# A two-layer decoder trunk on one core: order of two adding transfers, and how far ScalarE and VectorE prepare weights ahead inside the feed-forward units

## The reference, cut to what matters

```
hn = rms_norm(h, norm_ffn_g[layer])
h = h + (silu(hn @ ffn_w_gate[layer]) * (hn @ ffn_w_up[layer])) @ ffn_w_down[layer]     # 1024 -> 2816 -> 1024
```

## Time and profile before

| | us |
|---|---|
| median of 3 runs | 558.1 (558.05 to 558.82) |
| the profiled execution's own time | 559.87 |
| its span, first to last instruction | 558.0 |
| mean granted TensorE clock | 0.999 of full speed |
| PE busy / VectorE busy / ScalarE busy | 548.7 / 474.1 / 348.9 |

### The profile page before, as it was taken

How to read it: one execution, slowest core, us unless ns; L and a number is a source line. 1 busy time by engine, 2 the same in 40 slices (tenths; PEclk the granted TensorE clock), 3 DMA queues, 4 the chain that set the end, 5 groups by cost and what they waited for, 6 DMA issues and landing times.

```text
span 558.0 us, 7380 instructions
## 1 busy us (share of the span) xinstructions
PE 548.7 (98%) x2805; PEld 461.0 (83%) x2805; DVE 474.1 (85%) x564; ACT 348.9 (63%) x475; POOL 29.0 (5%) x70
## 2 busy tenths in 40 slices
PE   8999999999999999999999999999999999999996
PEld 7899978887888788888888888888788888878785
DVE  5769996798989999878798998977989898989765
ACT  6877664664767486655666366646576666748524
POOL 1200001100000010000000000001010000000000
PEclk9999999999999999999999999999999999999999
DMA  8995546845979879774469422409789697977102
GB/s 295 409 404 196 189 150 211 270 123 132 298 258 286 307 203 340 189 286 167 151 256 346 174 76 76 151 29 292 284 221 339 187 314 243 295 284 211 56 0 75
DMA packets 32867, 122.42 MB, mean 219 GB/s; under 512 B 3648, under 2 KB 4800, under 8 KB 30784
## 3 DMA queue, kind: packets, MB, share of 16 engines
q1 hardware_dynamic: 30384, 105.04, 49.8%
q0 software_dynamic: 2304, 16.78, 15.7%
q10 hardware_dynamic: 144, 0.14, 0.1%
HBM read 120.89 MB, written 1.05 MB: 219 GB/s over the span
## 4 chain that ended last, share of the span: by engine, by line
PE 71%; DVE 16%; DMA 5%; issue 4%; ACT 3%; POOL 0%; SPq 0%; DVEq 0%; ACTq 0%; POOLq 0%
PE bank L1792 12%; PE bank L1794 12%; PE bank L1793 12%; DVE w_lo L1133 7%; PE bank L2266 5%; PE bank L2265 5%; PE bank L2270 5%; PE bank L1903 4%; PE bank L2237 3%; DMA spare<-in_slabs 2%; DMA sixth_raw<-in_slabs 2%; PE bank L1906 2%; DVE raw L1597 2%; PE bank L2242 1%; ACT w_hi L682 1%
## 5 line engine op out<-in xcount | busy, mean ns | idle before, releaser
L1133 DVE TENSOR_TENSOR w_lo<-raw,w_hi 128x2048 fp32r<-128x2048 f32 (+2 forms) x71 | 156.2, 2211 | 21.5 <-ACT w_hi L682 21.0
L682 ACT ACTIVATE w_hi<-raw 128x2048 fp32r<-128x2048 f32 (+2 forms) x66 | 120.8, 1846 | 5.0 <-DMA raw<-in_slabs 2.8
L1792 PE MATMUL bank<-w_lo,yT_hi 128*128 128x512 f32 (+1 forms) x226 | 91.3, 404 | 2.2 <-DVE yT_lo L1690 1.6
L1794 PE MATMUL bank<-w_hi,yT_lo 128*128 128x512 f32 (+1 forms) x226 | 88.1, 390 | 0.0
L1793 PE MATMUL bank<-w_hi,yT_hi 128*128 128x512 f32 (+1 forms) x226 | 87.8, 389 | 0.0
L1133 DVE TENSOR_TENSOR w_lo<-sixth_raw,w_hi 128x2048 fp32r<-128x2048 f32 x22 | 50.3, 2285 | 5.0 <-ACT w_hi L682 5.0
L1792 PEld LDWEIGHTS bank<-w_lo,yT_hi 128*128 128x128 f32 x226 | 42.5, 188 | 13.1 <-DVE yT_lo L1690 4.2
L2265 PE MATMUL bank<-w_hi,forms_hi 128*128 128x512 f32 x128 | 50.4, 394 | 0.0
L1794 PEld LDWEIGHTS bank<-w_hi,yT_lo 128*128 128x128 f32 x226 | 42.4, 188 | 9.1
L2266 PE MATMUL bank<-w_hi,forms_lo 128*128 128x512 f32 x128 | 49.9, 390 | 0.0
L1793 PEld LDWEIGHTS bank<-w_hi,yT_hi 128*128 128x128 f32 x226 | 42.6, 189 | 7.4
(11 more groups left out here) (289 smaller groups left out, 1136.5 us busy)
## 6 DMA issues: line engine op xcount, KB each, us to landing
raw<-in_slabs SPq DMA_DIRECT2D x146, 512.0 KB, 7.7
sixth_raw<-in_slabs SPq DMA_DIRECT2D x28, 512.0 KB, 7.6
sixth_raw<-in_slabs POOLq DMA_DIRECT2D x6, 1024.0 KB, 11.3
spare<-in_slabs SPq DMA_DIRECT2D x12, 512.0 KB, 4.9
raw<-in_slabs POOLq DMA_DIRECT2D x6, 1024.0 KB, 8.8
spare<-in_slabs POOLq DMA_DIRECT2D x4, 1024.0 KB, 10.4
raw<-in_slabs SPq DMA_DIRECT2D x5, 256.0 KB, 4.6
h<-in_x SPq DMA_DIRECT2D x2, 512.0 KB, 6.7
```

The source lines that it names most:

```text
L682: A(w_of(s, c), raw_of(r, c), ACT.Copy).then_inc(hi_ready, 1)
L1133: V.tensor_tensor(w_of(s, c, 1), raw_of(preps[s][0], c), w_of(s, c).bitcast(F32), ALU.subtract).then_inc(lo_ready, 1)
L1792: T.matmul(o, st_hi, mv_lo, start=first, stop=False, skip_group_check=onto)
L1794: return T.matmul(o, st_lo, mv_hi, start=False, stop=last, skip_group_check=onto)
```

## The change

Three edits. GpSimd's program becomes third(2), third(4), fourth(2), third(6), fourth(4), third(8), fourth(6), fourth(8) in each layer, and the thirds count on two semaphores in turn. ScalarE rounds two more slabs (the down slab and T1) before the first unit, and in each unit works two slabs further ahead. VectorE takes T3's low part of the first unit after the activations' low part, takes the low part of the down slab before the first `seven_add`, and in units that have a follower puts `seven_add(a, 1)`, the next B11's low part and `block_add(a + 2, 0)` ahead of gates 0 and 1, and the next T3's and T2's low parts and `block_add(a + 2, 1)` ahead of `seven_add(a, 2)` and gate 3.

```
                 if (kind, a, b) in (("norm", 1, 1), ("norm", 3, 1)):
-                    for unit in SEVEN_AT[a // 2]:
-                        add_third(a // 2, unit)
-                        add_fourth(a // 2, unit)
+                    l, units = a // 2, SEVEN_AT[a // 2]
+                    add_third(l, units[0])
+                    for unit, following in zip(units, units[1:]):
+                        add_third(l, following)
+                        add_fourth(l, unit)
+                    add_fourth(l, units[-1])
...
                 at_hi_evac(3, 1, 1, 1)
+                next_hi(2)
...
                     seven_copy(a, 0)
-                    next_hi(2)
-                    if follows:
-                        seven_hi(a - 2, 3)
+                    next_hi()
                     seven_copy(a, 1)
-                    next_hi(4)
+                    next_hi(3)
                     seven_copy(a, 2)
+                    if leads:
+                        next_hi(2)
                     seven_silu(a, 0)
-                    if leads:
-                        next_hi()
                     seven_silu(a, 1)
                     seven_hi(a, 0)
                     seven_silu(a, 2)
-                    if leads:
-                        seven_hi(a, 1)
-                        next_hi(2)
-                        seven_silu(a, 3)
-                        seven_hi(a, 2)
-                        return
                     next_hi()
                     seven_hi(a, 1)
                     seven_hi(a, 2)
...
                 block_add(SEVEN_AT[l][0], 0)
-                split_los(f + 6)
                 activate(3, 1)
                 at_lo_evac(2, 0, 0, 1)
+                split_los(f + 6)
                 split_forms()
...
                     next_lo()
                     if follows:
-                        seven_act_lo(a - 2, 2)
                         seven_act_lo(a - 2, 3)
-                    next_lo(4)
+                    next_lo(5)
                     seven_add(a, 0)
-                    next_lo()
-                    seven_gate(a, 0)
                     if leads:
                         next_lo()
+                        seven_add(a, 1)
+                        seven_gate(a, 0)
+                        block_add(a + 2, 0)
+                        seven_gate(a, 1)
+                        seven_act_lo(a, 0)
+                        seven_gate(a, 2)
+                        next_lo()
+                        seven_act_lo(a, 1)
+                        next_lo()
+                        block_add(a + 2, 1)
+                        seven_add(a, 2)
+                        seven_gate(a, 3)
+                        seven_act_lo(a, 2)
+                        return
+                    seven_gate(a, 0)
                     seven_add(a, 1)
                     seven_gate(a, 1)
                     seven_act_lo(a, 0)
                     seven_gate(a, 2)
-                    if leads:
-                        block_add(a + 2, 0)
-                        seven_act_lo(a, 1)
-                        seven_add(a, 2)
-                        next_lo(2)
-                        seven_gate(a, 3)
-                        block_add(a + 2, 1)
-                        return
```

More of the change, by code:

```diff
@@ L370, in trunk @@
         block_sum = sem("block_sum")
-        third_added = sem("third_added")
+        third_added = [sem(f"third_added{i}") for i in range(2)]
         fourth_added = sem("fourth_added")
@@ L473, in trunk, with third_sum @@
         SUMS = ("t2", "t1")
+        def third_sum(l, a):
+            n = seven_no(l, a)
+            return third_added[n % 2], 16 * (n // 2) + 16
         sum_of_prep = {}
@@ L476, in trunk @@
             for a in SEVEN_AT[l]:
-                sum_of_prep[place["t3", l, a]] = (third_added, 16 * seven_no(l, a) + 16)
+                sum_of_prep[place["t3", l, a]] = third_sum(l, a)
                 sum_of_prep[place["t4", l, a]] = (fourth_added, 16 * seven_no(l, a) + 16)
@@ L638, in add_third @@
                 pool.wait_ge(raw_loaded[y], made)
-                nc.gpsimd.dma_start(raw_of(y), piece(n, 0, SLAB), accum_op=ALU.add).then_inc(third_added, 16)
+                nc.gpsimd.dma_start(raw_of(y), piece(n, 0, SLAB), accum_op=ALU.add)\
+                    .then_inc(third_sum(l, a)[0], 16)
             def add_fourth(l, a):
@@ L1032, in seven @@
                 def seven(a):
-                    follows, leads = a - 2 in SEVEN_AT[l], a + 2 in SEVEN_AT[l]
+                    leads = a + 2 in SEVEN_AT[l]
                     seven_copy(a, 0)
-                    next_hi(2)
-                    if follows:
-                        seven_hi(a - 2, 3)
+                    next_hi()
                     seven_copy(a, 1)
-                    next_hi(4)
+                    next_hi(3)
                     seven_copy(a, 2)
+                    if leads:
+                        next_hi(2)
                     seven_silu(a, 0)
-                    if leads:
-                        next_hi()
                     seven_silu(a, 1)
@@ L1591, in block_add @@
                     if m == 0:
-                        dve.wait_ge(third_added, 16 * seven_no(l, a) + 16)
+                        dve.wait_ge(*third_sum(l, a))
                     else:
```

## The result

The changed kernel is slower: 568.71 us (median of 4 runs, 567.52 to 569.05) against 558.46 of the kernel before on the same chip, a ratio of 1.0169 (95% interval 1.0147 to 1.0191). The sign of the forecast held and its size did not: 560.7 was forecast with 557.2 to 563.5 as range. The profiled execution has a span of 567.3 against 558.0, and a mean granted clock of 0.991 against 0.999.

A forecast was written before the change was run, and what follows sets the result against it. PE, busy 98% of the span, was taken as the bound, with only its stalls to win. Terms -1.32 - 2.03 + 5.0 + 1.0 = +2.65 us on 558.1 gave 560.7, range 557.2 to 563.5.

The forecast's parts named there:

- How long?: Layer 1's first unit: fourth(2), held behind third(4), lands at 419.95 instead of 416.55, so T4 is rounded 3.4 late.
- no slack to swallow them: Layer 1's first unit: the 3.4 come fully on top, as turn 0 is only just in time without them.
- Later fourths aren't held: Fourths after each layer's first: the next unit's third lands by 160 to 163, and fourth(4) is due at 163.
- the moved low part: Ahead of each layer's first unit: VectorE takes the activations' low part before T3's; 0.66 gained twice, -1.32.
- the late thirds' stall in layer 1: Third(8) of layer 1 no longer waits for a fourth to land; its stall of 1.41 goes.
- unit 6 of layer 0 and unit 4 of layer 1: Units 4 and 6: VectorE's new order makes quarter 0's low part 0.2 late; 0.25 a unit, +1.0 over both layers.
- the first unit's lateness without a hold: First unit of each layer: VectorE, in its new order after T4, delivers the low part 0.8 late to PE.
- ScalarE's lead at nothing: ScalarE rounding two slabs ahead issues the same roundings and slots allow it; costed at nothing.
- The long hold: Rival: both held transfers of layer 1 go at the thirds' pace, T4 8.5 late; +7.75, 565.85; chance 0.08.
- The short hold: Rival: both transfers of layer 1 take 7.8, T4 is 1.5 late; +0.75, 558.85; chance 0.22.
- the faster case: Rival: adding transfers land quickly, third(4) in 6.3 or less, so no hold; 557.35, or 555.75 if fourths are quick too; chance 0.12.
- VectorE late in every unit: Rival: the chain from copy 2 on VectorE takes 0.5 more in six units, 3 more; 563.7; chance 0.08.

The follow-up runs named there:

- two transfers in flight: The changed kernel with GpSimd's transfer scratch at 1024 instead of 512 and six small tiles moved: 565.21 us, 1.0090 against the kernel before.
- GpSimd's order alone: The kernel before with only the new order of thirds and fourths and the two semaphores: 562.72 us (561.2 to 569.09 over 11 runs), 1.0086.
- ScalarE's new order alone: The kernel before with the moved low part and, in layer 0 only, thirds ahead and ScalarE's new order, VectorE's order old: 571.72 us, 1.0214.

## Why the prediction was wrong

**The mechanism was right.** GpSimd gets no second adding transfer out before the one ahead has landed (0.23 after it, 0.25 taken), in whichever order; third(4) waits for its y and fourth(2) behind it; T4's rounding waits on ScalarE, and PE at B22 behind copy 2 and then at turn 0. With twice the scratch fourth(2) left before third(4) had landed: that the scratch holds it is shown by an experiment, not only argued.

**The step that failed is the size of the hold, "How long?"**, taken at 3.4 with 8.5 as its end. Measured against layer 0's first unit, which isn't held, T4 came 22.31 - 12.95 = 9.36 later, and the unit was 41.23 - 31.88 = 9.35 longer: "no slack to swallow them" was exact. The missing 6.0 add up from four figures: third(4) left at 404.12, not 402.2 (+1.9), as y's load, issued at 389.4 to 389.8, took up to 13.9 where the earlier trace rows had 12.9; it took 10.5, not 8.0 (+2.5), with a load that started 0.3 behind it, while in three runs in which that load started 1.5 behind it third(4) took 8.6 to 8.8; fourth(2) took 11.9, not 9.5 (+2.4); and the unheld T4 is 0.8 later than taken (404.42 + 12.95 = 417.37, not 416.55). I had given third(4) the fourths' time since "the queue has just run dry", and fourth(2) the slowest of theirs. But the fourths of the earlier trace rows had a start over the loads, and the held one hadn't: before, in layer 1, it left at 408.44, loads followed at 412.28 and 414.48, and it took 7.8; after, loads left at 411.31 and 413.51, ahead of it, and one at 415.71. The rule of round robin between queues (the Trainium skill, "DMA: Bandwidth & Descriptors", section on queues, rings and completion order), which I weighed and set aside, gave with the earlier trace rows an estimate of 11.5 for this transfer, and the trace's 11.9 is nearer to that than to my 9.5. It doesn't tell the cases apart, though: with loads that started 1.3 or more behind them, such transfers took only 7.8 to 10.1.

**"Later fourths aren't held" failed in layer 0.** Y of unit 6 was there at 155.9, not at 151; third(6) left then, and fourth(4) was held to 164.11 and landed 9.6 later. The new order has no room for that: unit 4 has +0.36 where -0.62 + 0.25 = -0.37 was summed.

**Terms that held:** the moved low part, -0.66 and -0.65 for twice -0.66; the late thirds' stall in layer 1, -1.26 for -1.41 + 0.25; unit 6 of layer 0 and unit 4 of layer 1, +0.17 and +0.19 for 0.25 each; the first unit's lateness without a hold, +1.06 for 0.8. ScalarE's lead at nothing can't be told as a term of its own: the two engines' orders stand or fall together.

Term by term the misses add up: 6.0 for the hold, 2 x 0.26 for first units, 0.73 for layer 0's unit 4, and -0.24 over the other three units, some +7.0; with +2.65 that is the +9.6 of the table.

**Rivals.** The long hold (+7.75, chance 0.08) was the nearest, and also too small. The short hold and the faster case are refuted: no adding transfer of these runs landed in less than 7.7, and the two that the hold is made of took 10.5 and 11.9. The Trainium skill, "DMA: Bandwidth & Descriptors", section on the anatomy of one DMA, would give an estimate of 4.4 us for such a transfer; no run here shows such a time for an adding one. VectorE late in every unit is refuted by units of 31.17 to 31.21.

**Open:** why fourth(2) took 9.4 with only the end of one load beside it, where others with as much took 7.7 to 8.3; why the steady units are 0.2 longer with two transfers in flight; what the four longer runs of GpSimd's order alone lost; and whether layer 1 could gain with y loaded earlier, which wasn't tried.

## What to carry to other kernels

Two transfers of one queue whose triggers are far apart are not independent: moving the one with the later deadline ahead is free only where its own input is there early, as in layer 0 with the old orders and not in layer 1. When a transfer is held, cost it at the speed it has at its new time, beside the loads that then run, and not at the time it used to take. And before tightening an order, read from the trace how late its input comes (here up to 14.15 after B11 was free in the old orders and up to 12.3 in the new); the slack that looks idle may be what absorbs the transfers' spread.

## What the runs showed of the hardware

- The time of an adding transfer of 1 MB goes with the loads around it, over all 208 in the thirteen traces. With no load beside it, or only one that landed within 3.0 of its start, it took 7.7 to 8.3 (9.4 once); with loads that start 1.3 or more after it, 7.8 to 10.1; with a load that starts within 1.3 of it, or that was out before it and landed 4.0 or more after its start, 10.5 to 12.9.
- With a scratch of 512 one such transfer is in flight; with 1024 two are (409.99 went out while the one of 403.90 landed at 412.7). They still land one behind another: in six pairs the first took 7.9 to 8.8, and the second landed 6.9 to 8.0 behind it, so the second took up to 12.5, and 15.1 once, from its issue.
- The granted clock fell after stops of PE of 7.22, 6.48, 5.17, 3.04 and 2.04 to its level of 1.2 GHz (0.51 in the window of after above), and stayed at 1.00 after stops of 3.39 and 1.84. After the same stop of 1.94 in three units of one run (ScalarE's new order alone) it fell in one and stayed in two. So the length of the stop alone doesn't decide.
